# The mean subtraction of three norms re-divided, the expert choice re-ordered, and tokens gathered for two experts at a time

## The reference, cut to what matters

```python
def layer_norm(x, g, b):
    mu = jnp.mean(xf, axis=-1, keepdims=True)
    var = jnp.mean(jnp.square(xf - mu), axis=-1, keepdims=True)
    return ((xf - mu) * lax.rsqrt(var + LN_EPS) * g + b).astype(x.dtype)
...
def moe_ffn(h, router, w1, w3, w2):
    logits = (h @ router).astype(jnp.float32)
    top_val, top_idx = lax.top_k(logits, TOP_K)
    top_w = jax.nn.softmax(top_val, axis=-1)
    gate = jnp.sum(jax.nn.one_hot(top_idx, N_EXPERTS) * top_w[..., None], axis=-2)
    out = gate[..., 0:1] * swiglu(h, w1[0], w3[0], w2[0])
    for e in range(1, N_EXPERTS):
        out = out + gate[..., e:e + 1] * swiglu(h, w1[e], w3[e], w2[e])
    return out
```

## Time and profile before

| | us |
|---|---|
| median of 3 executions (2034.21 to 2036.63) | 2035.61 |
| profiled execution, its own time | 2036.27 |
| its span, first to last instruction | 2034.3 |
| PE busy in it | 1950.3 (96%) |
| DVE busy | 1355.8 (67%) |
| ACT busy | 1062.5 (52%) |
| POOL busy | 85.1 (4%) |

### The profile page before, as it was taken

How to read it: one execution, slowest core, us unless ns; L and a number is a source line. 1 busy time by engine, 2 the same in 40 slices (tenths; PEclk the granted TensorE clock), 3 DMA queues, 4 the chain that set the end, 5 groups by cost and what they waited for, 6 DMA issues and landing times. The chain is left out here.

```text
span 2034.3 us, 25919 instructions
## 1 busy us (share of the span) xinstructions
PE 1950.3 (96%) x10571; PEld 1641.5 (81%) x10571; DVE 1355.8 (67%) x1550; ACT 1062.5 (52%) x1206; POOL 85.1 (4%) x149
## 2 busy tenths in 40 slices
PE   6999999899989999998999999999999999999995
PEld 5677879899976778887888888888888888888884
DVE  3744146644334643265597988979889798797986
ACT  2233233444322324244576776767767677676773
POOL 4002000200020011001000000000000000000000
PEclk9999999899989999999799999999999999999998
DMA  7223225355422232153399999999999999999992
GB/s 205 83 87 93 63 75 185 125 166 166 151 72 87 80 112 81 50 157 124 124 372 330 345 365 307 374 335 343 368 303 376 335 339 371 304 374 338 338 373 106
DMA packets 260479, 456.89 MB, mean 225 GB/s; under 512 B 32218, under 2 KB 111274, under 8 KB 260356
## 3 DMA queue, kind: packets, MB, share of 16 engines
q1 hardware_dynamic: 258966, 454.74, 65.2%
q10 hardware_dynamic: 1390, 0.44, 0.1%
HBM read 452.11 MB, written 3.04 MB: 224 GB/s over the span
## 5 line engine op out<-in xcount | busy, mean ns | idle before, releaser
L380 DVE TENSOR_TENSOR wl<-ring,wh 128x2048 fp32r<-128x2048 f32 x385 | 880.6, 2289 | 256.9 <-ACT wh L374 253.6
L374 ACT ACTIVATE wh<-ring 128x2048 fp32r<-128x2048 f32 x385 | 737.2, 1917 | 322.0 <-PE ps L349 322.0
L349 PE MATMUL ps<-hT,ring 128*128 128x288 f32 (+1 forms) x1376 | 360.7, 414 | 10.9 <-ACT hT L660 8.2
L349 PE MATMUL ps<-wh,xgh 128*128 128x512 f32 x896 | 355.3, 397 | 2.4 <-DVE wl L380 2.4
L349 PE MATMUL ps<-wh,xgl 128*128 128x512 f32 x896 | 350.1, 391 | 0.0
L349 PE MATMUL ps<-wl,xgh 128*128 128x512 f32 x896 | 349.7, 390 | 0.0
L349 PEld LDWEIGHTS ps<-hT,ring 128*128 128x128 f32 (+1 forms) x1376 | 253.7, 190 | 85.4 <-issue 15.5
L349 PEld LDWEIGHTS ps<-wh,xgh 128*128 128x128 f32 x896 | 168.7, 188 | 40.2 <-DVE wl L380 5.7
L349 PEld LDWEIGHTS ps<-wh,xgl 128*128 128x128 f32 x896 | 168.5, 188 | 36.2
L349 PEld LDWEIGHTS ps<-wl,xgh 128*128 128x128 f32 x896 | 168.9, 188 | 33.6
L349 PE MATMUL ps<-wh,gEh 128*128 128x512 f32 x448 | 143.5, 401 | 0.0
(11 more groups left out here) (405 smaller groups left out, 2412.7 us busy)
## 6 DMA issues: line engine op xcount, KB each, us to landing
ring<-in_moe_w SPq DMA_DIRECT2D x336, 1024.0 KB, 5.3
ring<-in_w_in SPq DMA_DIRECT2D x38, 1024.0 KB, 5.2
ring<-in_ffn_w SPq DMA_DIRECT2D x33, 1024.0 KB, 5.2
ring<-in_w_out SPq DMA_DIRECT2D x8, 1024.0 KB, 5.2
ring<-in_w_in SPq DMA_DIRECT2D x32, 128.0 KB, 3.1
ring<-in_w_oa SPq DMA_DIRECT2D x16, 256.0 KB, 3.9
ring<-in_w_ob SPq DMA_DIRECT2D x8, 512.0 KB, 4.9
resid<-in_x_prompt SPq DMA_DIRECT2D x1, 1024.0 KB, 5.2
```

Source lines behind the costliest of these rows:

```text
L349: ins = nc.tensor.matmul(*a, **k)
L374: nc.scalar.activation(wh[:, k % WS, :], ring[:, s:s + SLOT], ACT.Copy).then_inc(hi_ready, 1)
L380: ins = nc.vector.tensor_tensor(wl[:, k % WS, :], ring[:, s:s + SLOT], wh[:, k % WS, :].bitcast(F32), ALU.subtract)
```

## The change

**Norms.** POOL subtracts the mean from tiles 0 to 4 (five tiles, in that order), DVE from tiles 5 to 7, each right before that tile's multiplication; DVE's reciprocal stands ahead of all of it. Who makes the low parts in the dense mixer is as before (`HL_DVE = 4`).

```diff
-        XC_DVE = 4
+        XC_POOL = 5
...
             pool.wait_ge(nst_ready, 2 * q + 2)
-            for k in range(XC_DVE, KD):
+            for k in range(XC_POOL):
                 nc.gpsimd.tensor_tensor(hT[:, k, :], hT[:, k, :], mean, ALU.subtract).then_inc(xc_ready, 1)
...
-            dve.wait_ge(nst_ready, 2 * q + 2)
-            for k in range(XC_DVE):
-                c(nc.vector.tensor_tensor(hT[:, k, :], hT[:, k, :], mean, ALU.subtract))
             dve.wait_ge(nstd_ready, q + 1)
             c.link(nc.vector.reciprocal(rsd, sdev))
             for k in range(KD):
-                if k >= XC_DVE:
-                    dve.wait_ge(xc_ready, (KD - XC_DVE) * q + k - XC_DVE + 1)
+                if k < XC_POOL:
+                    dve.wait_ge(xc_ready, XC_POOL * q + k + 1)
+                else:
+                    c.link(nc.vector.tensor_tensor(hT[:, k, :], hT[:, k, :], mean, ALU.subtract))
                 nc.vector.tensor_tensor(tn[:, k, :], hT[:, k, :], rsd, ALU.mult).then_inc(tn_ready, 1)
```

```diff
-                        if ahead and 2 <= j < 2 + KD:
+                        if ahead and (2 <= j < 6 or 8 <= j < 12):
                             if j == 2:
-                                pe.wait_ge(oh_ready, i + 2)
-                            gather(pe, j - 2, htokh, 0)
-                            gather(pe, j - 2, htokl, 2)
-                        if j == 2 + KD:
+                                pe.wait_ge(oh_ready, (i + 1) // 2 + 1)
+                            if j == 8:
+                                pe.wait_ge(xg_ready, i + 2)
+                            gather(pe, j - 2 if j < 6 else j - 4, 2 * CAP)
+                        if j == 7:
                             turn_slots(pe, i)
...
-                def gather(pe, k, h, b):
+                def gather(pe, k, w):
-                    for t in range(NT):
-                        ins = rel.mm(ps[b + k // 4][:, CAP * (k % 4):CAP * (k % 4) + CAP], h[:, t, P * k:P * k + P],
-                                     oh[:, t, :], start=(t == 0), stop=(t == NT - 1))
+                    for h, b in ((htokh, 0), (htokl, 2)):
+                        for t in range(NT):
+                            ins = rel.mm(ps[b + k % 4 // 2][:, 2 * CAP * (k % 2):2 * CAP * (k % 2) + w], h[:, t, P * k:P * k + P],
+                                         oh[:, t, 0:w], start=(t == 0), stop=(t == NT - 1))
                     if k % 4 == 3:
                         ins.then_inc(ga_done, 1)
...
-                    if on and u in (34, 35, 38, 39):
-                        gathered(act, i + 1, (u - 34) // 4, u % 2)
+                    if on and i % 2 and u in (34, 35, 40, 41):
+                        gathered(act, (i + 1) // 2, (u - 34) // 6, u % 2, 2 * CAP)
...
-                            if u == 5 and e < NE - 1:
-                                dve.wait_ge(ga_done, 4 * e + 4)
-                                onehot(e + 1)
+                            if u == 5 and e % 2 and e < NE - 1:
+                                dve.wait_ge(ga_done, e + 1)
+                                onehot(e + 1, e + 2)
```

More of the change, by code:

```diff
@@ L95, in program @@
         ones = sb("ones", [P, P])
-        cumU = sb("cumU", [P, P])
-        blk = sb("blk", [P, P])
-        d16 = sb("d16", [P, P])
-        off16 = sb("off16", [P, P])
-        negL = sb("negL", [P, P])
-        negU = sb("negU", [P, P])
+        with ExitStack() as mem:
+            xgl = mem.enter_context(nc.sbuf_tensor("xgl", [P, KD, 2, CAP], F32R))
+        attn = sb("attn", [P, 6 * P + 2 * SEQ + NT * (PAST + DEC) + 64])
+        cumU, blk, d16, off16, negL, negU = [attn[:, P * j:P * j + P] for j in range(6)]
+        adm = attn[:, 6 * P:6 * P + 2 * SEQ].rearrange("p (i s) -> p i s", i=2)
+        ndist = attn[:, 6 * P + 2 * SEQ:6 * P + 2 * SEQ + NT * (PAST + DEC)].rearrange("p (i s) -> p i s", i=NT)
+        sel_ = attn[:, 6 * P + 2 * SEQ + NT * (PAST + DEC):]
         before = sb("before", [P, P])
@@ L2065, in _ @@
                     centred(pool, 0)
-                    for k in range(XC_DVE, KD):
+                    for k in range(HL_DVE, KD):
                         pool.wait_ge(h_ready, k + 1)
@@ L2165, in _ @@
                                                 ALU.mult, ALU.add).then_inc(hf_ready, 1)
-                    for k in range(XC_DVE):
+                    for k in range(HL_DVE):
                         dve.wait_ge(h_ready, k + 1)
@@ L2345, in hidden_out, with gathered, onehot @@
                                              scale=gslot[0:CAP]).then_inc(yh_ready, 1)
-                def gathered(act, i, h, low):
-                    v = ps[2 * low + h][:, 0:4 * CAP].rearrange("p (k t) -> p k t", k=4)
-                    if not low:
-                        act.wait_ge(ga_done, 4 * i + 2 * h + 1)
-                        nc.scalar.activation(xgh[:, 4 * h:4 * h + 4, :], v, ACT.Copy)
-                    else:
-                        act.wait_ge(ga_done, 4 * i + 2 * h + 2)
-                        nc.scalar.activation(xgl[:, 4 * h:4 * h + 4, :], v, ACT.Copy).then_inc(xg_ready, 1)
+                def gathered(act, p, h, low, w):
+                    act.wait_ge(ga_done, 2 * p + h + 1)
+                    for z in range(2):
+                        v = ps[2 * low + z][:, :].rearrange("p (k t) -> p k t", k=2)[:, :, 0:w]
+                        k = 4 * h + 2 * z
+                        ins = nc.scalar.activation((xgh, xgl)[low][:, k:k + 2, :, :].rearrange("p k e t -> p k (e t)")[:, :, 0:w], v, ACT.Copy)
+                    if low:
+                        ins.then_inc(xg_ready, 1)
                 def turned_view(g):
                     return ps[6 + g % 2][:, 0:4 * CAP].rearrange("p (c t) -> p c t", c=4)
-                def onehot(i):
-                    for t in range(NT):
-                        ins = nc.vector.tensor_scalar(oh[:, t, :], iota[:], posr[:, t, bass.ds(i, 1)], None, ALU.is_equal)
+                def onehot(*experts):
+                    for j, i in enumerate(experts):
+                        for t in range(NT):
+                            ins = nc.vector.tensor_scalar(oh[:, t, CAP * j:CAP * j + CAP], iota[:], posr[:, t, bass.ds(i, 1)], None,
+                                                          ALU.is_equal)
                     ins.then_inc(oh_ready, 1)
@@ L2478, in _ @@
                     for k in range(KD):
-                        if k % 4 == 0:
-                            pe.wait_ge(tok_ready, 1 + k // 4)
-                        gather(pe, k, htokh, 0)
-                        gather(pe, k, htokl, 2)
+                        if k in (0, 2):
+                            pe.wait_ge(tok_ready, 1 + k // 2)
+                        if k == 4:
+                            pe.wait_ge(xg_ready, 1)
+                        gather(pe, k, 2 * CAP)
                     for e in range(NE):
@@ L2496, in again @@
                     def again(i, e):
-                        pe.wait_ge(oh_ready, i + 1)
+                        pe.wait_ge(oh_ready, i - NE // 2 + 1)
                         for k in range(KD):
-                            gather(pe, k, htokh, 0)
-                            gather(pe, k, htokl, 2)
+                            if k == 4:
+                                pe.wait_ge(xg_ready, 2 * i - NE + 1)
+                            gather(pe, k, CAP)
                         up_units(pe, i, 0)
```

58 lines of the change are left out of this document (27 added, 31 removed).

## The result

The changed kernel takes 2022.7 us (median of 4 executions, 2020.15 to 2024.52), the kernel before 2036.12 beside it (4, 2034.21 to 2036.7): 0.9935 of it, 95% interval 0.9918 to 0.9952. It is faster by 13 us, where 28 were forecast, and outside the range given (2003.5 to 2015.0). The profiled execution took 2022.94 us, its span is 2021.1.

What follows compares the result with a forecast made beforehand. PE's stream was taken to bound the loop, and the chain through DVE the norms and expert choice. Terms -8.3 - 0.9 + 1.1 - 19.5 = -27.6 us from 2036.27 gave 2008.7, as a median 2008.0; range 2003.5 to 2015.

Steps and rivals of the forecast that it cites:

- The loop: Expert loop: dropped gathers less the costs in odd experts, 19.5 us less in all (bounds 22.9 and 17.3).
- transfers: Rival, even experts: weight transfers become the bound if the sustained rate is below 360 GB/s; at 350, 2022 us; 8%.
- columns: Rival, gather products: time goes with the columns, 16 us more in the loop and 10 ahead of it, 2034; 4%.
- clock: Rival, loop: PE's pauses let the half clock carry into the loop; at 80 us of it, 2048 us; 2%.
- The dropped gather: Down stages of experts 0, 2, 4 and 6: no gather on PE, 5.73 us each, 22.9 us less.
- The 256-column gather: Experts 1, 3 and 5: as many gather products, of 256 columns, 0.127 us each; 1.2 us more (bounds 0 and 1.6).
- The one-hots in the odd experts: DVE's queue at step 5: three one-hots more, mostly taken back; 0.2 us more in all (bounds 0 and 2.0).
- The hand-over: Odd expert to the next: PE stands 0.7 us behind ACT's step 41 split and copies, three times; 2.0 us more.
- Norms: Three turned norms: DVE's reciprocal and products start earlier, 2.7 + 2.8 + 2.8 = 8.3 us less (bounds 5.5 to 9.3).
- Expert choice: Choice before the first gather: PE's 1.53 us wait goes, three more one-hots cost 0.66; net 0.9 us less.
- First gather: Ahead of the loop: two blocks of 24 products of 256 columns, two 2.3 us pauses; 1.1 us more (0 to 4.9).
- the first rival: First gather: the clock stays low throughout, 3.8 us more than forecast, 2011.8 us; 20%.

Runs made afterwards that it cites:

- swapped: The changed kernel with `xgl` back right behind `xgh`, and `yh` and `yl` in the low memory instead: 2009.85 us.
- last kernel of group 2: The swapped kernel with gather tiles 4 to 7 moved to j = 8 and 9, and banks 4 to 7 used at the first gather: 2006.37 us.
- group 1: First four runs: changed kernel with `xgl` shifted 32 bytes (2018.07 us) or swapped (2009.85); kernel before with `xgl` low (2050.99) or norms change alone (2027.06).

## Why the prediction was right or wrong

**The loop: the step that failed.** The working took the four dropped gathers off a period whose other parts it held constant ("an even one would take 128.0 - 5.7 = 122.3 us"), and the move of `xgl` was set down as one that "changes no instruction there". So the time of the up stages was put at no change without a reason, and the runs showed 5.6 ns more on each of 2688 products and 11.1 us more in the loop (changed kernel against swapped), of the 13.6 that the loop fell short. No rival had it: transfers, columns and clock were considered, an address was not. None of the three explains it either. PE's waits for a split (`wl`) fell from 2.4 us to 0.9 over the loop, the granted clock in the up stage is 1.00, and the even experts' 124.0 us would have looked like the transfer rival (125.8) had not the down stage come out at 39.63 and the up stage been slow product by product. The sign that was given for being wrong, even experts above 124 us, came out on its edge (124.05, 123.95 and 123.94) and named transfers and DVE, which it was not.

With the address mended (swapped kernel) the loop takes 1004.85 us, 18.5 less than before, where the working had 19.5 and the clock's 1.5: even experts 122.54, 122.29 and 122.28 (forecast 122.3), odd ones 129.11 to 129.41 (129.5). The whole is 2009.85, in the range, 1.9 us from the forecast. That the whole is so near is partly luck: in its profiled execution the norms and the choice gave 3.0 us more than forecast, and the first gather 1.3 and the loop 2.5 less, and these nearly cancel. The bound of 17.3 for the loop was also added up wrongly: 22.9 less the upper bounds 1.6, 3.3 and 2.0 is 16.0.

**The parts of the loop.** The dropped gather: right, 39.63 us. (The single tile of rows 4 is not the 0.119 us a product that the working reads there but 0.62 / 6 = 0.103; the sum used the whole stage, so it stands.) The 256-column gather: in the last kernel of group 2, whose hand-over is free of copies, a stage with it takes 45.50 us and one without 39.60, so it costs 5.90 where the narrow one cost 5.73: 0.5 us more in all, not 1.2. The one-hots in the odd experts: 1.6 us (0.43, 0.57 and 0.57 in the swapped kernel, group 1) where 0.2 was taken, within the bound of 2.0; in the changed kernel the slow products hid them. The hand-over: right in kind and place, ACT's copies in its last step, but 0.48 us (start to start 0.70 against 0.23) where 0.7 was taken. ACT after:

```profile
1236.40 1.92 ACT L373 ACTIVATE wh<-ring 128x2048 fp32r<-128x2048 f32 x1 [0.57 <-PE ps L348]
1238.23 1.06 ACT L2355 ACTIVATE xgl<-ps 128x512 fp32r<-128x512 f32 x2
```

From the split's start to the next expert's first product it is 1239.34 - 1236.40 = 2.94 us, where the working had 3.17; this is the difference.

**Norms.** Right: 3.0 us each from variance to PE's first product, where 2.8 was said (3.1 without a collision). POOL's five tiles took 4.00 us, DVE's five products 2.73 where 5 x 0.38 = 1.9 would have been free of a collision, but only 0.2 us of that lay ahead of PE's start (1.45 us from the first product, 1.26 before). What the working did not have is the clock behind the second norm. Windows of the changed kernel there:

```profile
600.00:605.00 5.00, 3.76 (x8) 2.02 (x9) 4.92 (x10) 3.77 (x7) 4.58 (x8) 0.50 0.03 1
605.00:610.00 5.00, 5.00 (x22) 3.59 (x21) 1.28 (x6) 1.77 (x5) 4.11 (x12) 1.00 0.23 52
```

and of the kernel before, where PE starts later and the half clock lasts to about 609.4:

```profile
600.00:605.00 5.00, 0.00 (x0) 0.02 (x1) 4.96 (x7) 0.76 (x2) 4.58 (x8) 0.50 0.12 21
605.00:610.00 5.00, 4.99 (x12) 2.77 (x13) 2.20 (x7) 3.49 (x7) 4.17 (x11) 0.56 0.00 0
```

PE works 3.76 us of the low stretch instead of waiting through it, and the full clock is back before most of the work: that stretch gave 4.2 us, 1.2 more than the norm. The norms alone gave 8.7 us in all by the medians of the times, and 10.2 by the three stretches of the profiled execution, 1.2 of which is this clock.

**Expert choice.** Better than said: with norm 3 taken off (24.75 us to the first gather in the kernel with the norms alone), 1.75 us instead of 0.9. The three one-hots more cost what was said (DVE's six end 1.25 us after the first begins, three took 0.67). The rest is the clock again, which the working did not have: the counts now come in a stretch of full clock. PE's last six of them before, and after:

```profile
978.25 1.54 PE L2473 MATMUL ps<-experts,ones 128*128 128x8 f32 x6
```

```profile
968.50 0.93 PE L2477 MATMUL ps<-experts,ones 128*128 128x8 f32 x6
```

From the first count to the end of the last it is 2.72 us before (from 977.07) and 1.96 after (from 967.47): 1.53 + 0.76 - 0.58 = 1.7 less.

**First gather.** Between the forecast and the first rival. The two blocks were to take 5.3 and 3.0 us and the pauses 2.3 each; measured are 5.02, 4.35 and 2.43 twice. The second block's clock is 0.61: full clock in its beginning, then half again. And the 1.5 us that the first up unit was to win are not there: the clock is 0.66 in its first 5 us. Before the change it was 0.70 there. So the term is 4.0 us, not 1.1, near the end of its range (4.9). The pauses and the clock together cost the 3.9 us that the last kernel of group 2 takes back.

**The odds.** Faster by over 0.2% had 0.95 and came. That is little credit, since it came with half the gain. The range missed, since all its cases shared one assumption: that what the change does not issue stays as it is.

## What to carry to other kernels

When a tensor that feeds TensorE is moved in memory, compare its start address with that of the operand it meets, modulo 256 bytes, and look at the distance from product to product in stages that the change should not touch: here a pad of 96 bytes ahead of `xgl` (2007.94 us in one execution, against a median of 2022.7; loop 1004.6 against 1015.9) was worth more than the norms. And take a loop apart into its stages before blaming a resource: an even down stage right to the hundredth and an up stage slow in all units alike speak against a queue or a transfer.

## What the runs showed of the hardware

Products of 512 columns whose stationary and moving tiles all start at the same address modulo 256 bytes follow each other every 226.7 ns in an undisturbed unit (1.36 us for six), otherwise every 231 to 233. All three kinds of product slow down when only one stationary tensor is off. In the changed kernel, where only `xgl` is off, it is 234.5 ns beside the load of an `xgl` tile and still 233.6 and 231.9 beside the two loads of `xgh` (227.6 to 227.8 before). A conflict between the load of the next tile (0.188 us, begun 2 to 4 ns after the product it runs beside) and the reading of the moving side is a guess; by itself it would slow only the products beside a tile that is off, and these numbers say otherwise. The mechanism stays open, and so does why 32 and 160 bytes cost 5.4 to 5.7 ns (4.2 for `xgh` alone) and 128, 192 and 224 bytes 3.3 to 3.7. Distances of 64 and 96 were not tried in the up stage.

At full clock a product of 256 columns followed every 0.120 us in this kernel's gathers, a product of 128 columns every 0.110 to 0.115 inside a tile's six and every 0.119 by the length of the stage; at half clock it was 0.213 for both. So half the columns saved next to nothing. The Trainium skill, TensorE: Matmul & The Clock Gate, section "Back-to-back issue gap", gives a formula that makes it 56 and 109 ns at full clock, for a product by itself, and 81 ns for 128 columns in a stream of loads and products; the prediction took only the first. The trace is 11 ns above the formula for 256 columns, and for 128 above both figures.
